# Four changes of TensorE's program in a two-block hybrid transformer: gate inputs in four column groups, retention by row half, the inverse's last level two sides at once, the first feed-forward blocks as seven half products

## The reference, cut to what matters

```python
# stage even: sparse attention, and retention (4 heads, chunks of 128 tokens)
s = jnp.einsum('bnihd,bnjhd->bnhij', q, k) * decay          # scores of a chunk
intra = jnp.einsum('bnhij,bnjhe->bnihe', s, v)
cross = jnp.einsum('bnihd,ih,nbhde->bnihe', q, xi, s_prev)  # none for chunk 0
# stage odd: differential and latent attention
# stages ffn1 and ffn2, D_FF = 2816
a, b = jnp.split(x @ w_in, 2, axis=-1)
y = (jax.nn.silu(a) * b) @ w_out
# stage mix: HGRN2 branch, and gated delta branch (16 heads, chunks of 64 tokens)
beta = jax.nn.sigmoid(gb)                                   # gb, ga: 16 columns each of u @ w_in
g = -jnp.exp(a_log) * jax.nn.softplus(ga + dt_bias)
T = lax.linalg.triangular_solve(eye + A, eye, left_side=True, lower=True, unit_diagonal=True)
u = jnp.matmul(T, v * beta[..., None])
```

## Time and profile before

| what | value |
|---|---|
| runs of the kernel before | 2648.44, 2649.04, 2649.98 us, median 2649.04 |
| the profiled execution | 2648.66 us, its span 2646.9 us |
| TensorE busy | 2583.0 us, 98% of the span |
| VectorE busy | 1250.0 us, 47% |
| ScalarE busy | 657.5 us, 25% |
| GpSimd busy | 60.2 us, 2% |
| HBM traffic | 73 GB/s over the span |

### The profile page before, as it was taken

The page is one execution under the profiler, slowest core; times in us unless marked ns, Lnnn a source line. Parts: engine busy times, 40 slices in busy tenths (PEclk is TensorE's granted clock), DMA queues, the critical chain, the costliest instruction groups (busy, mean ns, idle before and its releaser), DMA issues.

```text
span 2646.9 us, 30821 instructions
## 1 busy us (share of the span) xinstructions
PE 2583.0 (98%) x12418; PEld 1696.8 (64%) x12418; DVE 1250.0 (47%) x2467; ACT 657.5 (25%) x1491; POOL 60.2 (2%) x116
## 2 busy tenths in 40 slices
PE   8999999999999999999999999999999999999999
PEld 3455547656478888744545845555556774788886
DVE  5733343444334456425464336657472543344564
ACT  2123331255200000133344043535343002000001
POOL 0000000000000000000000011101010000000000
...
DMA packets 120453, 194.71 MB, mean 74 GB/s; under 512 B 5148, under 2 KB 61272, under 8 KB 119416
## 3 DMA queue, kind: packets, MB, share of 16 engines
...
## 4 chain that ended last, share of the span: by engine, by line
PE 95%; ACT 2%; DVE 2%; issue 1%; DMA 0%; ACTq 0%; SPq 0%; DVEq 0%
PE psum L534 20%; PE psum L531 15%; PE psum L2344 15%; PE psum L420 9%; PE psum L2326 8%; PE psum L405 6%; PE psum L440 5%; PE psum L457 2%; PE psum L1198 2%; PE psum L1178 1%; PE psum L464 1%; PE psum L393 1%; PE psum L1186 1%; PE psum L2270 1%; PE psum L2545 1%
## 5 line engine op out<-in xcount | busy, mean ns | idle before, releaser
L2344 PE MATMUL psum<-weight_ring,h_t 128*128 128x512 f32 x896 | 409.1, 599 | 0.5 <-issue 0.5
L587 DVE TENSOR_TENSOR arena<-arena,psum 128x512 f32<-128x512 f32 x179 | 122.9, 686 | 348.8 <-PE psum L534 287.0
L2344 PEld LDWEIGHTS psum<-weight_ring,h_t 128*128 128x128 f32 x896 | 162.8, 192 | 163.6 <-issue 162.4
L420 PE MATMUL psum<-h_t,weight_ring 128*128 128x512 f32 x544 | 240.1, 602 | 2.6 <-ACTq L1955 1.1
L2326 PE MATMUL psum<-h_t,weight_ring 128*128 128x512 f32 x512 | 231.3, 594 | 0.3 <-issue 0.3
L534 PE MATMUL psum<-h_t,weight_ring 128*128 128x256 f32 x1024 | 228.2, 379 | 0.0
L531 PE MATMUL psum<-weight_ring,arena 128*128 128x256 f32 x992 | 222.2, 381 | 1.5 <-ACT arena L2758 1.5
L534 PEld LDWEIGHTS psum<-h_t,weight_ring 128*128 128x128 f32 x1024 | 194.5, 190 | 27.5 <-issue 1.3
L531 PEld LDWEIGHTS psum<-weight_ring,arena 128*128 128x128 f32 x992 | 189.6, 191 | 28.2 <-issue 2.2
L420 PEld LDWEIGHTS psum<-h_t,weight_ring 128*128 128x128 f32 x544 | 104.3, 193 | 134.5 <-issue 131.9
L405 PE MATMUL psum<-weight_ring,h_t 128*128 128x512 f32 (+1 forms) x384 | 167.4, 594 | 0.8 <-DVEq L1662 0.8
...
## 6 DMA issues: line engine op xcount, KB each, us to landing
...
```

What stands on the lines that cost most here:

```text
L420: last = pe.matmul(bank, slot[:, k, c:c + P], act[:, k, :], start=(k == 0), stop=(k == KD - 1))
L587: ins = dve.tensor_tensor(out, other, bank, op)
L2344: last = pe.matmul(bank, act[:, k, t * P:(t + 1) * P], slot[:, k, :], start=(k == 0), stop=(k == KD - 1))
```

## The change

Four parts, all in the order or form of TensorE's work and in what feeds it.

- The first block of each feed-forward stage becomes seven half products, in an order of its own (`SUMS_LATE`): p1, p2, p3, p5, p6, p7, p4. VectorE makes the block's weight sums first, then all four token sums, then joins the products. The separate last token sum goes.
- The gate inputs swap sides: the 32 weight columns become the stationary operand and 128 tokens the moving one. The four tiles go to four groups of 32 output partitions of one bank. ScalarE copies the result out in one operation, and after the second half of y_h one matmul turns it (`pe_delta_inputs_turned`), with one copy more.
- Retention's scores alternate between the row halves, and its outputs are issued as two inner matmuls, then two of the state, on two banks.
- The last level of the inverse is issued as x6 of units 0 to 7, then x6 of units 8 to 15 alternating with r6 of units 0 to 7, then r6 of units 8 to 15. Two of the four fillers behind it now stand before the last part.

```diff
+SUMS_LATE = ("p1", "p2", "p3", "p5", "p6", "p7", "p4")
...
-    for name in IN_TURN:
+    for name in SUMS_LATE if late_sums else IN_TURN:
         left, right = sides[name]
         bank = pe_fresh(K, pe, (key, name))
-        if name == "p6":
+        if name == ("p3" if late_sums else "p6"):
             pe.wait_ge(K.weights_summed, K.weight_sums["pe"])
-        if late_tokens and name == "p7":
+        if late_sums and name == "p5":
             pe.wait_ge(K.tokens_summed, K.token_sums["pe"])
         for q in range(2):
...
 def pe_ffn(K, pe, s):
     V = ffn_views(K)
-    blk = K.next_block()
-    pe.wait_ge(K.weight_landed[blk % SLOTS], K.landed_at[blk])
-    pe_feature_major(K, pe, (s, 0), K.h_t, [0, P, 2 * P, 3 * P], blk)
-    pe.wait_ge(K.tokens_summed, K.token_sums["pe"] + 1)
-    K.token_sums["pe"] += 2
-    for b in range(1, FFN_BLOCKS):
+    K.token_sums["pe"] += 1
+    for b in range(FFN_BLOCKS):
         blk = K.next_block()
         pe.wait_ge(K.weight_landed[blk % SLOTS], K.landed_at[blk])
-        pe_seven(K, pe, (s, b), blk, KD, K.h_t, V[f"weights{b % 2}"], V["tokens"], False, 2, b == 1)
+        pe_seven(K, pe, (s, b), blk, KD, K.h_t, V[f"weights{b % 2}"], V["tokens"], False, 2, b == 0)
...
-    opened *= FFN_BLOCKS - 1
+    opened *= FFN_BLOCKS
...
-    dve_token_sums(K, dve, K.h_t, KD, V["tokens"], but_last=True)
-    dve_weight_sums(K, dve, first_blk + 1, KD, V["weights1"], None, 2)
-    dve_last_token_sum(K, dve, K.h_t, KD, V["tokens"], ((s, 0), 3))
-    for n in range(2):
-        key = ((s, 0), 2 + n)
-        dve.wait_ge(K.full_of(key), K.turn(key))
-        dve.wait_ge(K.free_of(((s, 0), 2 + n)), K.turn(((s, 0), 2 + n)))
-    dve.tensor_copy(K.stat[:, 76:77], K.stat[:, 77:78]).then_inc(K.features_gated, 1)
...
+    dve_weight_sums(K, dve, first_blk, KD, V["weights0"], None, 2)
+    dve_token_sums(K, dve, K.h_t, KD, V["tokens"])
+    key = (s, 0)
+    both = V["gates"][:, 0, :].rearrange("p (q i t) -> p i q t", q=2, i=4)
+    dve.wait_ge(K.free_of((key, "p1")), K.turn((key, "p1")))
+    dve_product(K, dve, key, "p2", both[:, 0], pair(copied))
+    dve_weight_sums(K, dve, first_blk + 1, KD, V["weights1"], None, 2)
+    dve_product(K, dve, key, "p6", base, copied)
+    dve_product(K, dve, key, "p5", turned, base, keep=True)
+    dve_product(K, dve, key, "p3", both[:, 1], pair(turned))
+    dve_product(K, dve, key, "p7", base, base)
+    dve_product(K, dve, key, "p5", both[:, 3], pair(base))
+    dve_product(K, dve, key, "p4", both[:, 2], pair(base), op=ALU.subtract)
...
-        if b >= 3:
+        if b >= 2:
             dve.wait_ge(K.features_gated, done + b - 1)
         dve_product(K, dve, key, "p5", both[:, 3], pair(base))
-        used = ((s, b - 1), "p4") if b >= 2 else None
+        used = ((s, b - 1), "p4")
...
+    banks = [pe_fresh(K, pe, (s, "qk", t, par)) for par in range(2)]
+    for c in range(2):
+        for par in range(2):
+            p = 64 * par
+            ins = pe.matmul(banks[par][:, c * P:(c + 1) * P], V["qk_t"][p:p + 64, 2 + c, ts],
+                            V["qk_t"][p:p + 64, c, ts], start=True, stop=True)
+            if c == 1:
+                ins.then_inc(K.full_of((s, "qk", t, par)), 1)
...
 def pe_retention_outputs(K, pe, s, V, t):
     for par in range(2):
         pe.wait_ge(K.free_of((s, "qk", t, par)), K.turn((s, "qk", t, par)))
+    banks = [pe_fresh(K, pe, (s, "r", t, par)) for par in range(2)]
+    for c in range(2):
+        last = []
+        for par in range(2):
+            h, o = 2 * c + par, banks[par][:, c * P:(c + 1) * P]
+            last.append(pe.matmul(o, V["sd_t"][:, t * B_H + h, :], V["bv"][:, t, h * P:(h + 1) * P],
+                                  start=True, stop=(t == 0)))
+        for par in range(2) if t else ():
+            p, o = 64 * par, banks[par][:, c * P:(c + 1) * P]
+            last[par] = pe.matmul(o, V["qx_t"][p:p + 64, c, t * P:(t + 1) * P],
+                                  V["state"][p:p + 64, c * NT + t, :], start=False, stop=True)
-        last.then_inc(K.full_of((s, "r", t, par)), 1)
+        last[par].then_inc(K.full_of((s, "r", t, par)), 1)
...
         pe_seven(K, pe, (s, "y_h", half), blk, KD, V["o_t"], V[f"weights{half}"], V["tokens0"], True)
         if half == 0:
             pe_delta_inputs(K, pe, s, V)
+        else:
+            pe_delta_inputs_turned(K, pe, s, V)
...
 def pe_delta_inputs(K, pe, s, V):
 
     pe.wait_ge(K.inputs_landed, 16)
-    for t in range(NT):
-        bank = pe_fresh(K, pe, (s, "gab", t))
-        for k in range(KD):
-            last = pe.matmul(bank[:, 0:32], K.h_t[:, k, t * P:(t + 1) * P], V["gab_w"][:, k, :], start=(k == 0), stop=(k == KD - 1))
-        last.then_inc(K.full_of((s, "gab", t)), 1)
+    bank = pe_fresh(K, pe, (s, "gab"))
+    for k in range(KD):
+        for t in range(NT):
+            last = pe.matmul(bank[32 * t:32 * t + 32, 0:P], V["gab_w"][:, k, :], K.h_t[:, k, t * P:(t + 1) * P],
+                             start=(k == 0), stop=(k == KD - 1))
+    last.then_inc(K.full_of((s, "gab")), 1)
+
+
+def pe_delta_inputs_turned(K, pe, s, V):
+
+    pe.wait_ge(K.free_of((s, "gab")), K.turn((s, "gab")))
+    bank = pe_fresh(K, pe, (s, "gab_t"))
+    raw = V["gd_raw"].rearrange("p t c -> p (t c)")
+    pe.transpose(bank[:, 0:P], raw, K.const("ident")).then_inc(K.full_of((s, "gab_t")), 1)
...
-    for p in range(2):
-        bank = pe_fresh(K, pe, (s, "x6", g, p))
-        for u in units[8 * p:8 * p + 8]:
-            last = pe.matmul(bank[64:128, 64 * (u % 8):64 * (u % 8) + 64], lower[0:64, u, 64:128], tt[0:64, u, :],
-                             start=True, stop=True)
-        last.then_inc(K.full_of((s, "x6", g, p)), 1)
+    def x6(bank, u):
+        return pe.matmul(bank[64:128, 64 * (u % 8):64 * (u % 8) + 64], lower[0:64, u, 64:128], tt[0:64, u, :],
+                         start=True, stop=True)
+
+    def r6(bank, u):
+        return pe.matmul(bank[0:64, 64 * (u % 8):64 * (u % 8) + 64], V["x6"][64:128, u, :], rr[64:128, u, 64:128],
+                         start=True, stop=True)
+
+    bank = pe_fresh(K, pe, (s, "x6", g, 0))
+    for u in units[0:8]:
+        last = x6(bank, u)
+    last.then_inc(K.full_of((s, "x6", g, 0)), 1)
     pe_gdn_values(K, pe, s, V, g, 2)
     pe_take(fill, 4)
     pe.wait_ge(K.free_of((s, "r5", g, 1)), K.turn((s, "r5", g, 1)))
     pe.wait_ge(K.blocks_placed, 6 * g + 4)
-    for p in range(2):
-        pe.wait_ge(K.free_of((s, "x6", g, p)), K.turn((s, "x6", g, p)))
-        bank = pe_fresh(K, pe, (s, "r6", g, p))
-        for u in units[8 * p:8 * p + 8]:
-            last = pe.matmul(bank[0:64, 64 * (u % 8):64 * (u % 8) + 64], x6[64:128, u, :], rr[64:128, u, 64:128],
-                             start=True, stop=True)
-        last.then_inc(K.full_of((s, "r6", g, p)), 1)
+    pe.wait_ge(K.free_of((s, "x6", g, 0)), K.turn((s, "x6", g, 0)))
+    below, above = pe_fresh(K, pe, (s, "x6", g, 1)), pe_fresh(K, pe, (s, "r6", g, 0))
+    for u in units[0:8]:
+        last = x6(below, u + 8), r6(above, u)
+    last[0].then_inc(K.full_of((s, "x6", g, 1)), 1)
+    last[1].then_inc(K.full_of((s, "r6", g, 0)), 1)
     pe_gdn_values(K, pe, s, V, g, 3)
-    pe_take(fill, 4)
+    pe_take(fill, 2)
+    pe.wait_ge(K.free_of((s, "x6", g, 1)), K.turn((s, "x6", g, 1)))
+    bank = pe_fresh(K, pe, (s, "r6", g, 1))
+    for u in units[8:16]:
+        last = r6(bank, u)
+    last.then_inc(K.full_of((s, "r6", g, 1)), 1)
+    pe_take(fill, 2)
     pe.wait_ge(K.blocks_placed, 6 * g + 6)
...
-        for t in range(NT) if half == 0 else ():
-            key = (s, "gab", t)
-            act.wait_ge(K.full_of(key), K.turn(key))
-            act.copy(V["gd_raw"][:, t, :], K.bank(key)[:, 0:32]).then_inc(K.free_of(key), 1)
+        key = (s, "gab_t" if half else "gab")
+        act.wait_ge(K.full_of(key), K.turn(key))
+        act.copy(V["gd_raw"].rearrange("p t c -> p (t c)"), K.bank(key)[:, 0:P]).then_inc(K.free_of(key), 1)
```

47 lines of the change are left out of this document (9 added, 38 removed).

## The result

| what | before | after |
|---|---|---|
| runs, median | 2649.19 us (2648.44 to 2649.98) | 2629.34 us (2628.20 to 2630.12) |
| ratio | | 0.9923, 95% interval 0.9908 to 0.9938 |
| span of the profiled execution | 2646.9 us | 2628.2 us |

A forecast was written before the change was run, and what follows sets the result against it. TensorE, busy for 98% of the span, was taken to bound the kernel. Savings of 6.7, 9.65, 3.3 and 3.3 us, 22.95 in all, gave 2625.8 us; forecast range 2622 to 2629 (chance 0.71), with rivals 2620 to 2632.

The forecast's parts named there:

- The feed-forward blocks: First block of both feed-forward stages: seven products replace a plain block, 3.4 + 3.3 = 6.7 us saved, sum waits costed at nothing.
- The cover of 0.5 us: First feed-forward blocks: token sums ready at about 9.8 us, TensorE asks at 10.36 us at full clock, at least 0.5 us spare.
- The gate inputs: Gate inputs and y_h's second half: 64 matmuls in four column groups at 0.029 us each, 36.68 to 27.0 us, 9.65 saved.
- The turning matmul: Behind y_h's second half: two matmuls in the trace, 0.22 us plus 0.13 for the change of operands, 0.35 us.
- the two changes of shape at 0.2: Around the 64 gate-input matmuls: two changes of the array's shape, 0.2 us each, added to their 1.85 us.
- column groups don't overlap: Gate inputs: if the stationary operand changes with every matmul, 7.0 us instead of 1.85, +5.2, 2631 us; chance 0.06.
- Retention: Retention outputs in chunks 1 to 3: fewer shape changes and overlapping state parts save 1.1 us a chunk, 3.3 us in all.
- The inverse: Inverse's last level: x6 and r6 paired, 4.02 becomes 3.17 us in each of four groups, 3.3 us saved in all.
- the clock falls somewhere new: Sign of a wrong prediction, anywhere in the kernel: TensorE's clock falls at a new place; no size given.
- the lower clock stays, or it falls elsewhere: Rival: the clock still falls at y_h, or falls elsewhere, +2 to +5 us, 2628 to 2631; chance 0.10.
- The other rivals: Include inverse pairs not running beside each other, +3.3 to +3.8 us, chance 0.06; more saved, 2621 to 2623, chance 0.04.
- The slower one: Inverse: TensorE waits for VectorE's late copy of the second x6 behind two fillers, 2649 us and above; chance 0.01.

The follow-up runs named there:

- kept_busy: Changed kernel with extra matmuls of 512 columns, results not read, in TensorE's idle time at the stage ends; 2621.01 us, ratio 0.9892.
- the split run: Changed kernel with the inverse's last part cut in two: four r6, one filler, four r6, one filler; 2634.71 us.

## Why the prediction was right, and where it was off

**The feed-forward blocks** (forecast 6.7 us): 6.77 us measured, and the sums were ready 4.8 and 3.4 us ahead of their use, so costing them at nothing was right. The cover of 0.5 us that the prediction worked out for full clock was not put to use here, since the clock was 0.50 for the first 5.5 and 3.4 us of the two blocks; in kept_busy, at full clock, 0.8 us were left. What failed is the sentence's silence on everything behind the block: the part costs 1.4 us some 700 us later, by the order of the programs through the turn of banks. The prediction worked out what moves for VectorE's sums and for TensorE's waits on them, but not which bank each later job gets.

**The gate inputs** (9.65): 9.98. The 0.029 per matmul taken from two groups was right, 0.030 measured. The turning matmul cost 26.70 - 1.89 - 24.17 - 0.26 = 0.38 us, 0.35 had been said (the 0.13 us in it for a change of operands was the author's estimate, which no row shows), and the two changes of shape at 0.2 were not to be seen beside the 1.89; they are what makes the term 0.33 too small. The rival that column groups don't overlap is refuted: 0.030 us for each matmul in turn, 0.109 within one group. All four groups have the same 128 rows, and in the trace of the changed kernel four loads of 0.11 us each, one for each column group, start within 0.02 us of each other (1486.02 to 1486.04 us) while matmuls of 0.30 us from 1485.99 us on are in flight. In the plain blocks, too, where every load goes to the whole array, the loads of 0.19 us lie beside matmuls in flight, and 64 matmuls take no more than 0.43 us each.

**Retention** (3.3): 3.63. The two changes of shape for each c and the overlap of the state's parts came as said: four matmuls of 128 rows take 288.64 - 288.10 = 0.54 us and four of 64 rows 289.06 - 288.64 = 0.42. The scores gained nothing, as forecast.

**The inverse** (3.3): 2.29, the term that was mis-sized. The pairs overlap as said: 32 matmuls take 1.08 us. But eight x6 take 1.07 us instead of 1.0, the pairs 1.08 instead of 1.05, and the extra visit of r6 costs 1.27 with its two boundaries instead of 1.12: its start comes 1633.77 - 1631.95 = 1.82 us after that of four filler matmuls worth 1.72, it takes 1.07 itself, and the four behind it take 1.82 again. The price of a change of shape was put at 0.12 where the earlier trace rows had given 0.2; the split run measures 0.34 for one more visit with both its ends.

**The sum.** The four terms together were 22.95 and are 22.7. That they come so near is partly luck: the gate inputs and retention gave 0.33 us more than forecast each, and the inverse 1.0 less. The step that missed the other way is the one that was never written down: that the rest of the program takes the same time. It took 4.0 us more in the profiled execution. Of these, 1.2 stand between the first block and the gate inputs; there the wait for ScalarE that comes with the feed-forward part costs 1.4, and 0.4 less idle time without a named cause goes the other way. Another 1.8, at the start and behind the attention, lie within what profiles with the same instructions vary by. The last 1.05 stand between the gate block and the first x6. There the work is the same, with the same wait of 4.2 us, but the clock is low for longer. The same 15 us around that wait, before and after:

```profile
1593.00:1608.00 15.00, 10.78 (x33) 5.41 (x32) 14.07 (x32) 6.71 (x11) 2.79 (x4) 0.89 0.37 117
```

```profile
1579.00:1594.00 15.00, 10.78 (x31) 5.64 (x30) 14.07 (x32) 6.71 (x11) 2.79 (x4) 0.77 0.36 111
```

It is so in all seven profiles that have all four parts, 0.6 to 1.25 us in each, and in none of the seven others, so it comes with the change; why stays open.

The prediction named as a sign of being wrong that the clock falls somewhere new, and it does: in the changed kernel it falls to 0.50 at 1345 us for 3.4 us, behind an idle stretch of 2.0 us, where the kernel before keeps 1.00, and no longer at 1207 us. The rival "the lower clock stays, or it falls elsewhere", with 2628 to 2631, holds the measured time. Its first half was wrong: at the gate inputs and y_h the clock is 1.00. Its second half came true in part, for some 2.5 of the 4.0 us (1.41 + 1.05) are clock. So the range held, but the 2625.8 missed in part for the reason to which the prediction gave a chance of 0.10. The other rivals didn't happen. The slower one is far off: VectorE's copy started 0.10 us behind r6 in the trace, and TensorE never waited for it.
